# Second mixer's input weights: low parts of 60 chunks from GpSimd transfers that add the raw chunk to a negated rounded one

## The reference, cut to what matters

```python
def short_conv_mixer(h, buf, w_in, conv_w, w_out):
    proj = h @ w_in                      # h: 520 x 1024, w_in: 1024 x 8192, float32
    bg = proj[..., :D_SC]
    cg = proj[..., D_SC:2 * D_SC]
    xin = proj[..., 2 * D_SC:3 * D_SC]
    z = proj[..., 3 * D_SC:]
    conv, new_buf = causal_dwconv(cg * xin, buf, conv_w)
    y = bg * conv * jax.nn.silu(z)
    return y @ w_out, new_buf
```

## Time and profile before

| | |
|---|---|
| device time of three runs, us | 909.63, 909.87 (median), 912.41 |
| the profiled execution: span from first to last instruction, us | 906.4 |
| TensorE matmuls busy in the span | 881.7 us (97%), 7385 matmuls |
| VectorE busy | 608.0 us (67%) |
| ScalarE busy | 403.6 us (45%) |
| GpSimd busy | 147.1 us (16%) |
| mean granted TensorE clock | 0.993 of full |
| moved by DMA | 108.00 MB |

### The profile page before, as it was taken

The page is one execution under the profiler, slowest core; times in us unless marked ns, Lnnn a source line. Parts: engine busy times, 40 slices in busy tenths (PEclk is TensorE's granted clock), DMA queues, the critical chain, the costliest instruction groups (busy, mean ns, idle before and its releaser), DMA issues.

```text
span 906.4 us, 19336 instructions
## 1 busy us (share of the span) xinstructions
PE 881.7 (97%) x7385; PEld 870.2 (96%) x7385; DVE 608.0 (67%) x1039; ACT 403.6 (45%) x757; POOL 147.1 (16%) x95
## 2 busy tenths in 40 slices
PE   5999999999999999999999999999999999999996
PEld 5899999999999999989999999999999999999996
DVE  4579999969996999977575444544454555564533
ACT  6568677546855587643522222222211122253334
POOL 5404621433133404630000000000000000000000
PEclk9999999999999999999999999999999999999999
DMA  7336537644655366513343333333333333222212
GB/s 174 108 103 213 169 94 217 186 121 123 209 145 170 115 172 201 166 33 117 97 140 93 93 93 93 93 93 93 93 93 93 91 87 86 91 86 94 93 44 95
DMA packets 162993, 108.00 MB, mean 119 GB/s; under 512 B 5000, under 2 KB 155152, under 8 KB 162368
## 3 DMA queue, kind: packets, MB, share of 16 engines
q1 hardware_dynamic: 123876, 76.15, 28.7%
q10 hardware_dynamic: 38756, 30.61, 11.0%
q0 software_dynamic: 304, 0.48, 0.3%
HBM read 95.35 MB, written 12.14 MB: 119 GB/s over the span
## 4 chain that ended last, share of the span: by engine, by line
PE 76%; DVE 7%; issue 2%; ACT 2%; DMA 1%; DVEq 0%; POOLq 0%; POOL 0%; ACTq 0%
PE pair L1817 34%; PE bank L1817 20%; PE pair L1877 8%; PE pair L2081 5%; PE bank L2081 5%; DVE acc L1194 1%; PE bank L1970 1%; PE bank L1955 1%; PE bank L1719 1%; PE bank L1987 1%; DVE ybuf L1224 1%; DVE wlo L1064 1%; ACT em L711 1%; DMA abc<-a_rows 1%; DMA sample<-in_state_ssm 0%
## 5 line engine op out<-in xcount | busy, mean ns | idle before, releaser
L527 ACT ACTIVATE whi<-raw 128x1024 fp32r<-128x1024 f32 x136 | 143.7, 1057 | 353.9 <-PE bank L1817 137.3
L1817 PE MATMUL pair<-hhi,whi 128*128 128x260 f32 x1136 | 231.7, 285 | 0.2 <-DVE acc L1194 0.2
L1817 PE MATMUL pair<-hhi,wlo 128*128 128x260 f32 x1136 | 229.2, 283 | 0.0
L1817 PE MATMUL pair<-hlo,whi 128*128 128x260 f32 x1136 | 228.7, 283 | 0.0
L1064 DVE TENSOR_TENSOR wlo<-raw,whi 128x1024 fp32r<-128x1024 f32 x132 | 162.2, 1232 | 24.2 <-ACT whi L527 21.8
L1817 PEld LDWEIGHTS pair<-hhi,whi 128*128 128x128 f32 x1136 | 175.5, 189 | 1.9 <-DVE acc L1194 1.0
L1817 PEld LDWEIGHTS pair<-hlo,whi 128*128 128x128 f32 x1136 | 175.6, 189 | 0.0
L1817 PEld LDWEIGHTS pair<-hhi,wlo 128*128 128x128 f32 x1136 | 175.4, 189 | 0.0
L1817 PE MATMUL bank<-hhi,whi 128*128 128x260 f32 x512 | 103.1, 282 | 0.9 <-ACT sqs L512 0.9
L1817 PE MATMUL bank<-hhi,wlo 128*128 128x260 f32 x512 | 103.2, 283 | 0.0
L1817 PE MATMUL bank<-hlo,whi 128*128 128x260 f32 x512 | 103.0, 283 | 0.0
(11 more groups left out here) (256 smaller groups left out, 1306.7 us busy)
## 6 DMA issues: line engine op xcount, KB each, us to landing
raw<-in_sc_w_in SPq DMA_DIRECT2D x64, 512.0 KB, 4.0
raw<-in_ssd_w_in SPq DMA_DIRECT2D x40, 512.0 KB, 4.1
abc<-a_rows ACTq DMA_DIRECT2D x16, 512.0 KB, 4.2
sample<-in_state_ssm ACTq DMA_DIRECT2D x16, 512.0 KB, 4.4
out_new_ssm_s<-sample ACTq DMA_DIRECT2D x16, 512.0 KB, 4.9
raw<-in_ssd_w_out SPq DMA_DIRECT2D x16, 512.0 KB, 3.8
raw<-in_sc_w_out SPq DMA_DIRECT2D x16, 512.0 KB, 3.5
sample<-bc_rows ACTq DMA_DIRECT2D x4, 1024.0 KB, 6.2
```

Source lines behind the costliest of these rows:

```text
L527: act.activation(whi[:, slot, :], raw[:, slot % RAW, :], ACT.Copy).then_inc(hi_done, 1)
L1817: mm = pe.matmul(b, w[:, slot, k * P:(k + 1) * P], h[:, k, cols], start=(k == 0 and i == 0), stop=(k == KT - 1 and i == 2))
```

## The change

In the 15 turns j = 1 to 15 (chunks 60 to 119), the low part is no longer a subtraction on DVE. ACT writes the high part as before and then the negated raw chunk, rounded to fp32r, into `wlo`, and raises `neg_done`. GpSimd, whose queue is otherwise empty by then, waits for that and issues a transfer of `raw` onto `wlo` (both seen as float32) with an add: wlo becomes raw minus rounded raw. Its end raises one of four semaphores `sum_lo0` to `sum_lo3`. TensorE waits for that one instead of `lo_done`, and SP waits for it before it loads chunk n + 2 over the raw chunk. The chunks 56 to 59 and the output chunks 120 to 135 keep their subtraction. SP's two loops are written out.

```diff
@@ constants @@
+PARTS = 3, 1, 2, 0
+SUMMED_IN = 0, 1, 2, 3
+SUMMED = len(SUMMED_IN) * (TILES - 1)
@@ SyncE @@
+            def load1(j, m, src):
+                sp.wait_ge(hi_done, j * 4 + IN1 + m + (1 + SLOT - RAW))
+                sp.sem_inc(turnstile, 1)
+                before, last = (j, m - 2) if m > 1 else (j - 1, m + 2)
+                if before:
+                    sp.wait_ge(sum_lo[last], before * 16)
+                else:
+                    sp.wait_ge(lo_done, IN1 + SLOT + last + 1)
+                sp.sem_inc(turnstile, 1)
+                sp.dma_start(raw[:, m % RAW, :].rearrange("p (k n) -> p k n", k=KT), src).then_inc(raw_in[m % RAW], 16)
...
+            for m, part in enumerate(PARTS):
+                load(IN1 + m, IN1 + m, w_in1[:, :, part * DI:part * DI + P])
+            for j in range(1, TILES):
+                for m, part in enumerate(PARTS):
+                    load1(j, m, w_in1[:, :, j * P + part * DI:(j + 1) * P + part * DI])
@@ GpSimd @@
+            for j in range(1, TILES):
+                for i, m in enumerate(SUMMED_IN):
+                    pool.wait_ge(neg_done, len(SUMMED_IN) * (j - 1) + i + 1)
+                    pool.dma_start(wlo[:, m, :].bitcast(F32), raw[:, m % RAW, :], accum_op=ALU.add).then_inc(sum_lo[m], 16)
@@ ScalarE, block1 @@
                     high(j * 4 + (IN1 + m + SLOT), m, j * 32 + ((IN1 + m + SLOT) // RAW + 1) * 16)
+                    if m in SUMMED_IN and not ahead:
+                        act.activation(wlo[:, m, :], raw[:, m % RAW, :], ACT.Copy, scale=-1.0).then_inc(neg_done, 1)
@@ VectorE, block1, the same at m = 1, 2 and 3 @@
-                    low(j * 4 + (IN1 + SLOT), 0)
+                    if ahead * jj:
+                        low(j * 4 + (IN1 + SLOT), 0)
@@ TensorE, project @@
                 pe.wait_ge(hi_done, n + (SLOT + 1))
-                pe.wait_ge(lo_done, n + (SLOT + 1))
+                if turn is None:
+                    pe.wait_ge(lo_done, n + (SLOT + 1))
+                else:
+                    pe.wait_ge(sum_lo[slot], turn * 16)
```

More of the change, by code:

```diff
@@ L262, in hybrid_step @@
         direct_st = sem("direct_st")
+        neg_done = sem("neg_done")
+        sum_lo = {m: sem(f"sum_lo{m}") for m in SUMMED_IN}
         turnstile, turnstile_p = sem("turnstile"), sem("turnstile_p")
@@ L322, in _, with load_out @@
                     load(n, n, w_in0[:, :, col:col + P])
[L324 to L332, removed]
+            def load1(j, m, src):
[8 more added lines that the diff above has]
+                sp.dma_start(raw[:, m % RAW, :].rearrange("p (k n) -> p k n", k=KT), src).then_inc(raw_in[m % RAW], 16)
+            def load_out(half, c):
+                n = OUT1 + half * 8 + c
+                sp.wait_ge(hi_done, n + (1 + SLOT - RAW))
+                sp.sem_inc(turnstile, 1)
+                if n < OUT1 + RAW:
+                    sp.wait_ge(sum_lo[c + 2], 16 * (TILES - 1))
+                else:
+                    sp.wait_ge(lo_done, n + (1 + SLOT - RAW) - SUMMED)
+                sp.sem_inc(turnstile, 1)
+                sp.dma_start(raw[:, c % RAW, :].rearrange("p (k n) -> p k n", k=2),
+                             w_out1[:, 2 * c:2 * c + 2, half * 512:(half + 1) * 512]).then_inc(raw_in[c % RAW], 16)
+            for m, part in enumerate(PARTS):
[3 more added lines that the diff above has]
+                    load1(j, m, w_in1[:, :, j * P + part * DI:(j + 1) * P + part * DI])
+            for half in range(2):
+                for c in range(8):
+                    load_out(half, c)
             sp.dma_start(outs["new_ssm_conv_s"][0, :, 0:PRE0 - 1, :], ins["state_ssm_conv"][0, :, 1:PRE0, :]).then_inc(direct_st, 16)
@@ L1662, in block1 @@
                     dve.tensor_copy(dec[:, :, 0:PRE1], cst1[:, ds(j, 1), :, :].squeeze(1)).then_inc(cs1_done, 1)
-                    low(j * 4 + (IN1 + 1 + SLOT), 1)
+                    if ahead * jj:
+                        low(j * 4 + (IN1 + 1 + SLOT), 1)
                     dve.wait_ge(sl_done, j + 1)
@@ L1685, in block1 @@
                     dve.wait_ge(c2_done, j + 1)
-                    low(j * 4 + (IN1 + 2 + SLOT), 2)
+                    if ahead * jj:
+                        low(j * 4 + (IN1 + 2 + SLOT), 2)
                     for r in range(ahead * jj):
@@ L1692, in block1 @@
                     dve.tensor_tensor(yt[:, TH:T], bank[7][:, 0:TH], c2[:, TH:T], ALU.mult).then_inc(bg_free, 1)
-                    low(j * 4 + (IN1 + 3 + SLOT), 3)
+                    if ahead * jj:
+                        low(j * 4 + (IN1 + 3 + SLOT), 3)
             with dve.Fori(0, STEPS) as J:
@@ L1805, in project_first, with project @@
                 mm.then_inc(proj_done, 1)
-            def project(n, slot, b0, b1, h_ready=None):
+            def project(n, slot, b0, b1, h_ready=None, turn=None):
                 pe.wait_ge(hi_done, n + (SLOT + 1))
-                pe.wait_ge(lo_done, n + (SLOT + 1))
+                if turn is None:
+                    pe.wait_ge(lo_done, n + (SLOT + 1))
+                else:
+                    pe.wait_ge(sum_lo[slot], turn * 16)
                 for k in range(KT):
@@ L2066, in out_phase @@
                         pe.wait_ge(hi_done, half * 8 + (base + c + SLOT + 1))
-                        pe.wait_ge(lo_done, half * 8 + (base + c + SLOT + 1))
+                        pe.wait_ge(lo_done, half * 8 + (base + c + SLOT + 1 - SUMMED))
                         pe.wait_ge(y_hi, half * 16 + (2 * c + 2))
@@ L2096, in part @@
                         pe.wait_ge(tail_c, 1)
-                    project(j * 4 + (IN1 + m), m, bank[2 * m][:, 0:TH], bank[2 * m + 1][:, 0:TH], h_ready)
+                    project(j * 4 + (IN1 + m), m, bank[2 * m][:, 0:TH], bank[2 * m + 1][:, 0:TH], h_ready, None if first else j)
                 pe.wait_ge(z_free, j + 1)
```

## The result

The changed kernel takes 934.88 us (median of four runs, 933.51 to 936.06), the kernel before on the same chip 910.07 us (909.63 to 912.41): a ratio of 1.0264 with a 95% interval of 1.0243 to 1.0285. The medians are 24.8 us apart. The sign and the range of the prediction hold. The size does not: 54 us were forecast. The span of the profiled execution is 934.2 us, that of before 906.4. The profiled execution itself took 936.06 us, 1.9 above its span; the prediction had put 3.5 us there, from a median.

What follows compares the result with a forecast made beforehand. TensorE alone was taken to bound the loop. Chunk 60's lateness and 29 buffer turns gave 30 s - 150 = 42 us at s = 6.4, plus 12 for overlap: 54 us on 909.87, so 964 us, range 913 to 1018.

Steps and rivals of the forecast that it cites:

- What bounds the kernel: In the loop only TensorE sets the time, at 5.76 us a chunk; nobody else does.
- VectorE's relief: 60 subtractions, 73.5 us, leave VectorE in the loop; never waited for, so worth nothing.
- Where the loss would be: Chunk 60 late by 4.7 us, then each raw buffer's turn too long by 1.3 us, with TensorE pausing per chunk pair.
- The term s: Time from issue to landing of GpSimd's adding transfer, taken as 6.4 us, with 4.9 and 8.2 kept as bounds.
- The row of 512 KB: Trace row of a ScalarE-issued transfer from SBUF to HBM, 4.9 us, used as the bound on s from below.
- The neighbours of s: Other terms of a raw buffer's turn: passes 2.02, hand-over 0.1, next load's issue 0.22, load 4.03, overlap 0.4 us.
- the ring: Raw buffers' turn in the loop: 6.4 + s, 12.8 us at s = 6.4, against TensorE's 11.52 for two chunks.
- The sum: Loss up to chunk 118, 29 turns behind chunk 60: 30 s - 150, 42 us, plus 12 for overlap, 54 us.
- The second rival: Slightly slower: s from 4.3 to 5.5 us with little overlap, loss mostly chunk 60's, 912.5 to 925 us; chance 17%.
- The clock: TensorE's pauses in the loop may drop its clock, some 2 us, but within pairs waiting anyway; it lengthens nothing.
- Behind chunk 118: After the loop's sums, low parts come from VectorE again; a buffer's turn of 6.5 us is short enough.
- The signs I named: TensorE waits about 55 us for sums in some 30 pauses of 1.3 to 2 us, first near 4.7; `wlo<-raw` at 6.4.

Runs made afterwards that it cites:

- four buffers: The changed kernel with four raw buffers in place of two, two dead tiles serving as the third and fourth: 919.41 us, ratio 1.0111.
- side traffic: The kernel before plus 60 adding 512 KB transfers by GpSimd between two unused tiles, which no other engine waits for: 911.14 us, ratio 1.0001.
- repaired end: The changed kernel with ScalarE's last-turn Silu and yhi ahead of output chunks' high parts, and VectorE's low parts of 120 and 121 moved: 933.11 us, ratio 1.0252.
- sums from turn 8 on: The changed kernel with low parts by subtraction before turn 8 and by GpSimd's transfers only in turns 8 to 15: 923.11 us, ratio 1.0139.
- moved low parts: The changed kernel with VectorE's low parts of output chunks 120 and 121 moved behind the last turn's convolution: 939.39 us, ratio 1.033.

## Why the prediction was right in sign and wrong in size

- **What bounds the kernel; VectorE's relief.** Right. TensorE alone sets the loop's time, and the relief is worth nothing (1.0002). The passes on ScalarE and the traffic on TensorE's side are free, as it said.
- **Where the loss would be.** Right in place. Chunk 60 is late, high parts wait for raw loads, SyncE for GpSimd, and TensorE pauses once a pair of chunks, 26 times in all. With four buffers the loop's pauses go, as a ring demands.
- **The term s.** Mis-sized, and by choice of row: I took 6.4 us from the 1024 KB transfer. In chunk 60's buffer the sum lands in 4.6 us, and SyncE's next load starts 4.7 us behind GpSimd's issue; the median of all sixty landings, 5.1, lies between this buffer's and the other's 5.4. The row of 512 KB at 4.9, my lower bound, was the near one. The Trainium skill (Collectives: The Full Stack, The bandwidth ceiling) was my reason to pass it over. Its point that the second read costs is compatible with the runs, 5.1 us with the add and 2.9 without, but none separates the read from the adding. The error was to conclude that the sum then takes as long as 1024 KB to HBM.
- **The neighbours of s.** Mis-sized the other way. At s = 4.7 the prediction's own formula gives a loss of 3.0 us at chunk 60 and none in the ring, 913 us. It takes the load at 4.03 us with 0.4 of overlap in a whole turn, where the next high part comes 5.1 us behind the load's issue, and the hand-over to GpSimd at 0.1 where it is 0.3. The prediction put the overlap between nothing and 1.8 us a turn and took a value near nothing, since "the transfers here overlap for a small part only". That step failed: the loads of this buffer lie beside the other buffer's sums for 3.2 of their 5.1 us. By terms: predicted 2.02 + 0.1 + 6.4 + 0.22 + 4.03 + 0.4 = 13.2 us, measured 2.0 + 0.3 + 4.7 + 5.1 = 12.1. The sum was 2 us too long and the rest 0.9 too short.
- **The sum.** The form holds with the measured terms: 3.2 us of pause at chunk 60 and 29 x (12.11 - 11.54) = 16.5 are 19.7 us; 20.0 were lost up to the end of the loop. With 13.2 instead of 12.11, 29 turns give 32 us too many; chunk 60 gives 1.5 too many (4.7 for 3.2), and the end of the loop, below, 5 too few. That is about the difference between 54 and 24.8. A tenth of a microsecond in a turn is 3 us in the time, which is why errors of 1 to 2 us decided so much. The second rival had the right s and the time 912.5 to 925; its "little overlap" is what failed.
- **The clock.** It was said to cost nothing within the loop. That it fell is plain (0.54 behind the pause of 3 us), and it cost chunk 60 2.65 us. But the ring ran on meanwhile, and the chunks 62 to 65 have no pause at all; 16.5 us for the turns less these 2.65 is about the 14.2 counted. So in the changed kernel the step holds. With four buffers no ring takes it back: chunk 60 takes 7.3 us for 5.77, and these 1.5 us stay in the time. Behind the loop it cost another 1.5 us that the prediction did not have.
- **Behind chunk 118.** "A buffer's turn of 6.5 us is short enough" failed. The turn is short, but the queues of ScalarE and VectorE hold the last turn's gating behind the high and low parts of the output chunks, and these come as late as the ring. That is 3.5 us, and 5 with the lower clock behind it, a fifth of the measured loss, and the prediction had nothing for it.
- **The signs I named.** About 30 pauses of 1.3 to 2 us: 26, all but one of the later ones under 1 us. 55 us in sum: 10.5 in the view of waits, 15.4 from start to start. First one near 4.7 us: 3.0. `wlo<-raw` at 6.4: 5.1. I had named a raw load of over 5 us beside the sum as a mark of error, and in chunk 60's buffer it was 5.1 up to the next high part. The sum had 4.43 for it.

What stays open: which part of the 2.2 us between copy and add is the second read and which the add itself, since no run reads twice without adding; and how the 3.5 us of waiting behind the loop split between ScalarE's and VectorE's order.

## What to carry to other kernels

For each ring of buffers write down the whole turn (fill, every reader, hand-overs, refill) beside the time in which its consumer uses up the ring, and multiply the difference by the turns. When a step of 1.2 us on an engine is replaced by a transfer of 5 us, an engine's busy time falls and a ring with room can become the bound; the relief counts only if somebody waited for that engine. A transfer's price in such a sum is the one beside the others of the same loop, not alone. Work in queue order behind a late ring is late even after the ring has ended.

## What the runs showed of the hardware

- A transfer of 512 KB from SBUF to SBUF, 128 rows, issued by GpSimd: 2.9 us to landing as a copy, 5.1 us (4.5 to 6.2) with an add onto the target. GpSimd's issue takes 0.53 and 0.86 us. The Trainium skill (DMA: Bandwidth & Descriptors, Anatomy of one DMA) would give an estimated 3.2 us for the copy and 4.4 with the bytes of two reads; the traces show 0.3 less and 0.7 more.
- Loads from HBM and sums slow each other. The median load goes from 4.0 us in the kernel before to 4.5 in the changed one and 4.7 beside the side traffic. In the changed kernel sums land in 4.6 us in one buffer and 5.4 in the other; with four buffers, where two loads can run beside a sum, in 5.6 to 6.8.
- From the end of ScalarE's pass to GpSimd's issue it takes 0.3 us.
- A pause of TensorE of 3.0 us was followed by 5.8 us at 1.2 GHz, one of 4.1 us by 3.4 us, and so was one of 2.0 us (repaired end); one of 4.5 us (sums from turn 8 on) and one of 7.3 us (moved low parts) each went with 10.2 us. The 25 short pauses of up to 1.3 us were followed by none. The stretch of 5.8 us made chunk 60 last 2.65 us longer, that of 3.4 us cost 1.5.
